# Down projections of block 2 by Strassen's scheme over eight pairs of input rows, for six of eight output tiles

## The reference, cut to what matters

```
def swiglu(x, w_gu, w_down):                 # w_gu 1024 x 5632, w_down 2816 x 1024
    g, u = jnp.split(x @ w_gu, 2, axis=-1)
    return (jax.nn.silu(g) * u) @ w_down
...
x = layer_norm(ALPHA * x + 0.5 * swiglu(x, ffn1_w_gu[l], ffn1_w_down[l]), ln1_g[l], ln1_b[l])
```

## Time and profile before

| | us |
|---|---|
| median of 3 runs | 3413.47 (3411.47 to 3414.45) |
| the profiled execution, its own time | 3413.02 |
| its span | 3411.2 |
| PE busy | 3383.5 (99%) |
| PE weight loads busy | 2917.4 (86%) |
| DVE busy | 2519.0 (74%) |
| ACT busy | 1600.6 (47%) |
| POOL busy | 433.6 (13%) |

### The profile page before, as it was taken

One profiled execution on the slowest core, in us unless ns is written; L12 is line 12 of the kernel. 1 busy time (PEld: TensorE's weight loads), 2 busy tenths in 40 slices (PEclk: granted clock), 3 DMA queues, 4 the chain that ended last, 5 costly groups with the idle time before them and its releaser, 6 DMA issues.

```text
span 3411.2 us, 50605 instructions
## 1 busy us (share of the span) xinstructions
PE 3383.5 (99%) x19622; PEld 2917.4 (86%) x19622; DVE 2519.0 (74%) x3115; ACT 1600.6 (47%) x2183; POOL 433.6 (13%) x305
## 2 busy tenths in 40 slices
PE   9999999999999999999999999999999999999998
PEld 6888889988788888998899876899889988679986
DVE  8999568934999657963797388898288937978954
ACT  5555444423565444542444256544254524664433
POOL 3333010001333210001000120200020003120002
PEclk9999999999999999999999999999999999999999
DMA  3112334333221233332443221333333232123332
GB/s 127 62 62 68 108 120 161 100 117 117 69 68 62 88 127 124 131 123 98 146 147 118 93 81 56 123 117 100 119 124 112 100 123 89 60 85 138 100 123 99
DMA packets 98845, 357.23 MB, mean 105 GB/s; under 512 B 10960, under 2 KB 14544, under 8 KB 96976
## 3 DMA queue, kind: packets, MB, share of 16 engines
q1 hardware_dynamic: 85824, 305.68, 26.7%
q10 hardware_dynamic: 12816, 48.70, 3.8%
HBM read 321.83 MB, written 16.78 MB: 99 GB/s over the span
## 4 chain that ended last, share of the span: by engine, by line
PE 87%; issue 4%; DVE 3%; POOL 2%; ACT 1%; POOLq 1%; DMA 1%; DVEq 0%; SPq 0%; ACTq 0%
PE ps L2496 15%; PE ps L2498 14%; PE ps L2497 14%; PE ps L2557 10%; PE ps L2558 10%; PE ps L2556 10%; PE sc L2496 3%; PE sc L2497 3%; PE sc L2498 3%; POOLq L1452 1%; PE ps L2735 1%; DVE w_lo L1510 1%; PE sc L2810 1%; POOL DE L1454 1%; POOL Y L1447 1%
## 5 line engine op out<-in xcount | busy, mean ns | idle before, releaser
L1510 DVE TENSOR_TENSOR w_lo<-raw,w_hi 128x1024 fp32r<-128x1024 f32 x369 | 476.9, 1292 | 472.0 <-ACT w_hi L757 448.2
L757 ACT ACTIVATE w_hi<-raw 128x1024 fp32r<-128x1024 f32 x369 | 390.1, 1058 | 805.8 <-PE sc L2498 402.8
L2496 PE MATMUL ps<-h_hi,w_hi 128*128 128x512 f32 x1352 | 566.3, 419 | 10.9 <-DVE w_lo L1510 5.9
L2498 PE MATMUL ps<-h_hi,w_lo 128*128 128x512 f32 x1352 | 529.3, 391 | 0.0
L2497 PE MATMUL ps<-h_lo,w_hi 128*128 128x512 f32 x1352 | 528.5, 391 | 0.0
L870 ACT ACTIVATE w_hi<-raw 128x1024 fp32r<-128x1024 f32 x204 | 216.4, 1061 | 386.6 <-PE ps L2558 209.2
L2557 PE MATMUL ps<-h_lo,w_hi 128*128 128x256 f32 x1272 | 359.9, 283 | 0.0
L2556 PE MATMUL ps<-h_hi,w_hi 128*128 128x256 f32 x1272 | 359.7, 283 | 0.0
L2558 PE MATMUL ps<-h_hi,w_lo 128*128 128x256 f32 x1272 | 359.7, 283 | 0.0
L2496 PEld LDWEIGHTS ps<-h_hi,w_hi 128*128 128x128 f32 x1352 | 254.7, 188 | 84.7 <-issue 29.9
L2497 PE MATMUL ps<-hid_lo,w_hi 128*128 (+1 forms) x792 | 308.2, 389 | 0.0
(11 more groups left out here) (393 smaller groups left out, 7647.9 us busy)
## 6 DMA issues: line engine op xcount, KB each, us to landing
raw<-wts SPq DMA_DIRECT2D x471, 512.0 KB, 3.3
S<-wts SPq DMA_DIRECT2D x51, 512.0 KB, 3.3
A<-wts SPq DMA_DIRECT2D x51, 512.0 KB, 3.3
x<-parked ACTq DMA_DIRECT2D x7, 2048.0 KB, 8.7
h_hi<-early_hi ACTq DMA_DIRECT2D x15, 512.0 KB, 3.9
h_lo<-early_lo ACTq DMA_DIRECT2D x15, 512.0 KB, 3.5
parked<-x ACTq DMA_DIRECT2D x24, 256.0 KB, 2.0
parked<-x ACTq DMA_DIRECT2D x3, 2048.0 KB, 8.7
```

The lines of the kernel that those rows point to most:

```text
L757: act(w_hi[:, s].rearrange("p a b -> p (a b)"), raw[:, s, :], ACT.Copy).then_inc(s_whi, 1)
L1510: tt(w_lo[:, s].rearrange("p a b -> p (a b)"), raw[:, s, :], w_hi[:, s].rearrange("p a b -> p (a b)").bitcast(F32), ALU.subtract).then_inc ...
L2496: mm(out, w_hi[:, s, b, :], hi, start=start, stop=False, skip_group_check=True)
L2498: return mm(out, w_lo[:, s, b, :], hi, start=False, stop=stop, skip_group_check=True)
```

## The change

For the four feed-forwards of block 2 (`DOWN_QUAD_FFS`) the first 6 hidden rows (`DOWN_PLAIN`) are taken one by one as before. The other 16 rows are 8 pairs (an even and an odd row), and six of the eight output tiles are 3 pairs of tiles. For each pair of tiles the product of [2 tiles] x [even rows, odd rows] x [tokens 0 to 255, tokens 256 to 511] is made in seven products of blocks instead of eight, each of 8 x 3 matmuls with 256 columns (`down_by_quads` on PE). The last two tiles are made directly, in four chunks of 24 matmuls with 512 columns.

Three sums of hidden blocks are needed as moving operands (T2, N3, N4, each 128 x 2048), with hi and lo parts; they are formed once per feed-forward. `token_difference` writes the difference of the token halves of the even row over its second half already in the gate and up stage. Four weight sums per pair of tiles are formed on DVE as in the gate and up stage. Products are not combined in PSUM alone: when one is finished, DVE adds it with its sign straight onto the halves of x that it belongs to (`take`, 10 per pair of tiles), and the six plain rows are added by `take_plain` for all eight tiles before that.

The core of the diff:

```diff
+DOWN_QUAD_FFS = (2, 3, 4, 5)
+N_DOWN_QUADS = 3
+DOWN_PLAIN = 6
+DOWN_PAIRS = (FT - DOWN_PLAIN) // 2
...
+        DOWN_BANKS = ((5, 4, 6), (0, 1, 2), (5, 6, 7))
...
+            def load_down_quads(f, c0):
...
+                        eng.wait_ge(s_hidl, FT * (f + 1))
+                        eng.dma_start(SD1[:], a21).then_inc(e_a21, 16)
+                        eng.dma_start(A22[:], a22).then_inc(e_a22, 16)
+                        eng.wait_ge(s_wlo, c0 + 1)
+                        eng.dma_start(raw[:, 0, :], a11).then_inc(s_raw[0], 16)
...
+            def down_quads_hi(f, pair0):
...
+                def token_hi(out, src, i):
+                    eng.wait_ge(e_sum, down_token_sum(f, i))
+                    act(out, src, ACT.Copy).then_inc(e_hi, 1)
...
+                split_hi(pair0 + 1, 0)
+                token_hi(TD_hi[:], TD[:], 5)
+                split_hi(pair0 + 1, 1)
+                split_hi(pair0 + 2, 0)
+                token_hi(ND_hi[:], ND[:], 7)
+                split_hi(pair0 + 2, 1)
+                eng.wait_ge(s_used, c0 + 1)
+                a11_hi(0)
+                s2_hi(0)
+                eng.wait_ge(e_used, down_tile(f, KT - 1))
+                s1_hi(0)
+                token_hi(FD_hi[:], FD[:], 9)
...
-                down_rows(pair0)
...
+                def token_difference(q):
+                    if token_differences(f, q + 1) > token_differences(f, q):
+                        eng.wait_ge(e_ev, ev_done(f, q, TIMES1))
+                        tt(gates[:, 0, HALF:], gates[:, 0, HALF:], gates[:, 0, 0:HALF], ALU.subtract).then_inc(e_ev, 1)
...
+                if down_quads(f):
+                    second_product(n_quads - 1)
+                    split_lo(pair0 + FT, 1)
+                    token_difference(n_quads - 1)
...
+            def down_quads_lo(f, pair0, n, scale, centre):
...
+                for k0 in (0, 4):
+                    first_sums(0, k0)
+                for k0 in (0, 4):
+                    first_sums(1, k0)
+                split_lo(pair0 + 1, 0)
+                for k0 in (0, 4):
+                    first_sums(2, k0)
+                token_sum(ND[:], down_rows_of(hid_hi, 0, 0).bitcast(F32), TD[:], ALU.subtract, 5)
+                split_lo(pair0 + 1, 1)
+                token_lo(0, TD_lo, TD, TD_hi)
+                token_sum(ND[:], ND[:], down_rows_of(hid_lo, 0, 0).bitcast(F32), ALU.add, 6)
+                split_lo(pair0 + 2, 0)
+                eng.wait_ge(e_lo, down_token(f, 0))
+                token_sum(FD[:], down_rows_of(hid_hi, 1, 0).bitcast(F32), TD[:], ALU.subtract, 6)
+                token_lo(1, ND_lo, ND, ND_hi)
+                split_lo(pair0 + 2, 1)
+                token_sum(FD[:], FD[:], down_rows_of(hid_lo, 1, 0).bitcast(F32), ALU.add, 8)
+                s3(0)
+                s1(0)
+                block_lo(0, raw[:, 0, :])
+                eng.wait_ge(s_park, back(f))
+                take_plain(0)
+                s2(0)
+                take_plain(1)
+                block_lo(1, raw[:, 0, :])
+                for j in range(2, 5):
+                    take_plain(j)
+                block_lo(2, SD1[:])
+                for j in range(5, KT):
+                    take_plain(j)
+                token_lo(2, FD_lo, FD, FD_hi)
...
+            def down_by_quads(pair0, f, centre):
...
+                for i in range(DOWN_PLAIN):
+                    s = i % 2
+                    eng.wait_ge(s_wlo, c0 + i + 3)
...
+                        last = three(ps[n][:], s, n, hid_hi[:, i, :], hid_lo[:, i, :], i == 0, i == DOWN_PLAIN - 1)
...
+                for q in range(N_DOWN_QUADS):
+                    b = PRODUCTS * q
+                    X, Y, Z = DOWN_BANKS[q]
+                    eng.wait_ge(e_ev, (down_taken(f, 3), down_taken(f, 6), down_take(f, 0, DOWN_TAKES - 1))[q])
+                    product(b, Y, *hid(0, 0), True)
+                    eng.wait_ge(e_lo, down_token(f, 0))
+                    product(b + 1, X, TD_hi, TD_lo, True)
+                    product(b + 2, Z, *hid(0, 1), True)
+                    eng.wait_ge(e_lo, down_token(f, 1))
+                    eng.wait_ge(e_ev, down_take(f, q, 3))
+                    product(b + 3, X, ND_hi, ND_lo, False)
...
```

More of the change, by code:

```diff
@@ L66 @@
 SCRATCH_ROW = 10
+DOWN_QUAD_FFS = (2, 3, 4, 5)
+N_DOWN_QUADS = 3
+DOWN_PLAIN = 6
+DOWN_PAIRS = (FT - DOWN_PLAIN) // 2
+DOWN_TOKEN_SUMS = 10
+DOWN_TAKES = 10
 HALF = SEQ // 2
@@ L1468, in layer_norm @@
                 eng.wait_ge(s_xp, n * N_PLAIN + N_CENTRE)
-                eng.tensor_tensor(centre_parts[:], x[:, order[0], :], x[:, order[1], :], ALU.add).then_inc(s_xs, 1)
+                parts = centre_parts if i == 1 else centre_down
+                eng.tensor_tensor(parts[:], x[:, order[0], :], x[:, order[1], :], ALU.add).then_inc(s_xs, 1)
                 add_squares(5 + n, 1, 4)
@@ L2217, in layer_norm @@
+            def layer_norm(i, L, c0, order, evacuate, hv, folded_to=(), f=None):
                 n = 3 * L + i
@@ L2246, in take_folded, with centre_early, take_first_half, take_last @@
                         stt(to, to, -1.0, ps[4][:], ALU.mult, ALU.mult).then_inc(done, 1)
-                for j, k in enumerate(order):
+                def centre_early(q):
+                    if q == 0:
+                        eng.wait_ge(s_cs, n + 1)
+                    centre(CENTRED[q]).then_inc(s_xc, 1)
+                def take_first_half(j):
+                    k = order[j]
+                    eng.wait_ge(s_used, c0 + j + 1)
+                    part = x[:, k, HALF:]
+                    stt(part, ps[k][:, 0:HALF], 0.5 / ALPHA, part, ALU.mult, ALU.add).then_inc(e_ev, 1)
+                def take_last(j):
+                    eng.wait_ge(s_used, c0 + j + 3)
+                    eng.wait_ge(e_ev, down_take(f, N_DOWN_QUADS, j - 6))
+                    evacuate(order[j]).then_inc(s_xc, 1)
+                if f is not None:
+                    down_quads_lo(f, (c0 - DOWN_ROWS) // 2, n, 0.5 / ALPHA, centre_early)
+                    centre(4).then_inc(s_xc, 1)
+                    centre(5).then_inc(s_xc, 1)
+                    centre(6)
+                    centre(7)
+                    centred_lo(0)
+                    eng.drain()
+                    take_first_half(6)
+                    split_chunk(c0 + 6)
+                    centred_lo(1)
+                    centred_lo(2)
+                    take_first_half(7)
+                    split_chunk(c0 + 7)
+                    for q in range(3, 6):
+                        centred_lo(q)
+                    take_last(6)
+                    split_chunk(c0 + 8)
+                    centred_lo(6)
+                    take_last(7)
+                for j, k in enumerate(order if f is None else ()):
                     if j >= N_PLAIN:
@@ L2880, in centre_sum @@
                 eng.wait_ge(s_xs, n + 1)
-                mm(ps[4][:], ones_r[:], centre_parts[:], start=True, stop=True).then_inc(s_cs, 1)
+                parts = centre_parts if n % 3 == 1 else centre_down
+                mm(ps[4][:], ones_r[:], parts[:], start=True, stop=True).then_inc(s_cs, 1)
             def sums(n, last_tile):
@@ L3137, in feed_forward @@
     rows = w_down.reshape(FT, P, KT, P)
+    if down_quads(f):
+        first = rows[DOWN_PLAIN:].reshape(DOWN_PAIRS, 2, P, KT, P).transpose(1, 3, 2, 0, 4)
+        blocks = [first[half, DOWN_ORDER[2 * q + tile]] for q in range(N_DOWN_QUADS)
+                  for half, tile in ((0, 0), (1, 0), (1, 1), (0, 1))]
+        blocks += [first[half, DOWN_ORDER[j]] for half in range(2) for j in (6, 7)]
+        return [gu.reshape(N_GU, P, CHUNK, P), rows[:DOWN_PLAIN], np.stack(blocks)]
     last = rows[DOWN_ROWS:].transpose(2, 1, 0, 3)[list(DOWN_ORDER)]
```

345 lines of the change are left out of this document (324 added, 21 removed).

## The result

The changed kernel takes 3436.96 us (median of 4 runs, 3436.79 to 3437.41), the kernel before 3413.67 us (median of 4 runs beside it). The ratio is 1.007, with a 95% interval of 1.0059 to 1.0082: slower by 0.7%. The profiled execution took 3437.41 us, its span is 3435.6 us, 24.4 more than before.

A forecast was written before the change was run, and what follows sets the result against it. PE's own time, busy 99% of the span, was taken as the bound. 3413.0 - 19.8 (PE's saving) + 32.6 (start) + 6.8 (clock) = 3432.6, forecast as a median of 3433 us, range 3418 to 3445.

The forecast's parts named there:

- PE's saving, 4.9 us per feed-forward: Down projection: 504 half-width matmuls (60.4 us) replace 288 of 512 columns (65.3 us), 19.8 us saved in all four.
- The start, 8.0 us and 8.2: Ahead of the first product PE waits for DVE: 8.0 us lost in the first feed-forward, 8.2 in each other, 32.6 in all.
- The walk: DVE's queue counted instruction by instruction from the first down matmul; first product at 40.65 us, 5.65 after PE ran dry.
- Waits at plain rows 2 and 3: Expected sign in the profile: PE waits some 1 us for DVE at each of these rows of the down projection.
- The inside of the pairs: In each pair of tiles DVE's 16.4 us, up to 19, fit within PE's 20.1 us, without waits in later pairs.
- Product 3: Tightest place in the first pair of tiles: the take it needs comes at 49.2 us, PE at 49.3.
- The clock, 6.8 us: At or just after each first product PE's clock falls to 0.50: 1.7 us each, 6.8 in four; bounds nothing and double.
- Token differences and tail, nothing: Gate-and-up token differences fall where DVE waits: nothing, or 10 us without that cover; the last two tiles cost as before.
- The tail rival: In the last two tiles DVE's takes come 2 us late four times, product 3 0.5 us late: about 3447; 12%.
- the skill's rule: GpSimd and two-input VectorE instructions exclude each other: 23.4 us of work for 21.8 in the last two tiles, 3438.
- that the work hides: Rival: the sums of the start run beside the plain rows and PE keeps its saving, 3394; 6%.
- that the clock stays up: Rival: PE stalls ahead of the first product but its clock is not touched, 3426; 17%.

The follow-up runs named there:

- the kernel whose clock was kept up: The change plus 20 unread 512-column matmuls ahead of the first product of the first pair in each feed-forward; 3426.71 us, ratio 1.0038.
- the experiment with the waits per bank: The change with the wait for four takes ahead of the first product split over the banks, one take per product; 3435.46 us, ratio 1.0064.

## Why the prediction was right

- **PE's saving, 4.9 us per feed-forward.** Right. In the kernel whose clock was kept up, the three pairs took 60.4 to 60.6 us from the first product on, where 504 x 0.1198 is 60.4; the same stretch took 65.6 before. So the saving is 5.1 us, 20.5 in all. PE's busy time fell by only 5 us, since the slow clock is in it; I have not taken the rest of that difference apart.
- **The start, 8.0 us and 8.2.** Right in all four: first product at 40.61 and 40.84 after T0, predicted 40.65 and 40.85. Against the 32.7 of the kernel before that is 32.4 us in all. The walk stands in the rows shown within 0.1 us: first half sum 6.16 (6.1), S3 at 31.54 (31.6), take 0 at 35.15 (35.15), take 2 at 39.23 (39.3). Waits at plain rows 2 and 3 were 1.1 us or less, 5.39 us for take 3.
- **The inside of the pairs.** Right: no wait in any pair. The 256-column take, which had no row, took 0.418 us in the mean; I had put 0.42 between the ends of the earlier trace rows. Product 3 was as tight as said: with PE 4.7 us earlier it waited 3.5.
- **The clock, 6.8 us.** Right in kind, small in size: 2.04 to 2.58 us each time, 9.3 in all. I took the cost of the one 3.2 us stretch that the trace showed; here 4.5 to 5.7 us of PE's work ran at 0.50. Adding matmuls gave back 8.5 us, which shows it.
- **Token differences and tail, nothing.** Right for the first: narrowing them changed nothing. Right for the tail itself: 21.79 us without a wait. Not quite nothing behind it: h_lo took 1.47 us in the mean over the kernel, POOL's sum of squares ended 2.06 us behind PE's last tile where it was 1.62 before, and PE lost 0.45 us behind three of the four down projections. The tail rival had put 2 us, and 1.6 by the skill's rule.
- **What I left out.** 4.5 us between the down projections, less 1.1 ahead of the first and 0.3 behind the fourth. Of the 4.5, 1.3 are the waits for POOL's squares; the rest stands mostly behind late loads of A22, varies from 0 to 3.7 us over thirteen kernels, and its cause is open.

Sum: -20.5 + 32.4 + 9.3 = 21.2, measured 21.3 in the stages; 3.1 outside. The profiled execution is 4.8 us above the 3432.6 of the forecast: the clock took 2.5 us more, the 3.1 outside the stages were not in it, and against that PE saved 0.7 more and the start cost 0.2 less.

The rivals: that the work hides was wrong, as the experiment with the waits per bank showed; that the clock stays up was wrong at 5.4 us of idle time and half right at 2.3; the tail took 1.3 us, not 14.

## What to carry over

Before a scheme that trades PE columns for sums goes into another stage, put the sum engine's busy time per stage next to PE's: here DVE went from 41% to 87% of the stage, and a saving of 4% of PE's time was gone. Then walk the queue of the engine that prepares the first operand, instruction by instruction from the last stage's end, because an average over the stage doesn't show a start for which nothing is ready. If it is late, order its queue by deadline and fill its waits for loads before anything else (22 us here), and give none of its two-input work to GpSimd.
